# Handing the low parts of the output weights from VectorE to GpSimd, from weights that ScalarE scales in place

## The chip, the cores and the metric

The kernel runs on one core of a Trainium2 chip. The metric is the time of one launch on the device in microseconds (us); less is better. A core has TensorE (matrix products, PE in the profile; its weight loads are PEld), VectorE (DVE), ScalarE (ACT), GpSimd (POOL) and SyncE (SP), which here issues all DMA transfers.

## What is computed

One decoder layer over 2048 positions of width 1024, in float32: an RMSNorm, one input projection whose columns feed two groups of 512 channels, an output projection with residual, then a feed-forward block and a final RMSNorm.

```python
h = rmsnorm(x, norm_mix)
proj = h @ w_in                                 # x_lru, g_lru, v_cm, g_cm: 512 columns each
c = causal_depthwise_conv(x_lru, conv4_w, conv4_b)
y_lru = rg_lru(c, ...) * gelu(g_lru)            # gated linear recurrence over the positions
d = causal_depthwise_conv(v_cm * sigmoid(g_cm), dw31_w, dw31_b)
y_cm = silu(layernorm(d, cm_ln_g, cm_ln_b))
y = concat(rmsnorm(y_lru, out_norm_lru), rmsnorm(y_cm, out_norm_cm))
x = x + y @ w_out
h = rmsnorm(x, norm_ffn)
x = x + (silu(h @ w_gate) * (h @ w_up)) @ w_down
return rmsnorm(x, norm_final)
```

## The kernel before, in words

**Split products.** Every large product is made from operands split in two: a high part in the type fp32r, and a low part, the difference between the float32 value and the high part. `product` (L1328) adds three matmuls per chunk of 128 rows: high by high (L1334), high by low (L1335), low by high (L1336).

**Stages.** Stage 1 runs over 8 units (`UNITS`: two halves of 1024 positions by 4 blocks of 128 channels). A unit has two pairs of projections (`project`, 16 pairs in all, `PPAIRS`). For each pair SyncE loads raw weights into one of two buffers `w_raw`, ScalarE writes the high part (`split_hi`, L701) and GpSimd the low part (`split_lo`, L544). Around the projections: the short convolution and the gates (ScalarE, GpSimd), the recurrence as a scan (VectorE, `scan`, L1143), and the long convolution of 31 taps (VectorE, `conv31`, L1186), one instruction of 128x1024 per tap, whose running sum lies in PSUM. Stage 2 is the output projection: 16 row tiles of 128 positions, each in two groups (the LRU channels, then the others) of two PSUM banks with 12 matmuls each; the rows are added to the residual on VectorE (`add_row`, L1167), normed (`hn`, L1259) and transposed by TensorE (`turn_h2`, L1481). Stage 3 is the feed-forward block.

**The output weights.** They are four blocks (`WOQ`), n = 0 to 3, of 2 x 128 rows by 1024 columns, and use the same two buffers `w_raw` as pairs 16 to 19. `load_w_out` (L383, SyncE) waits until the low part of the block two before it is made (`s_wlo`). `w_out_hi` (L917, ScalarE) multiplies the raw rows by the gains of the output norms (`w_out_gain`) and writes `wo_hi`, one instruction per 128x1024. `w_out_lo` (L1157, VectorE) makes `raw * gain - wo_hi`, also one instruction per 128x1024. The kernel places the four calls by hand into the last long convolution, `conv31(7)`, ahead of the taps 12, 14, 17 and 19 (`W_OUT_AT`, L267). In the same convolution stand the scan of unit 6 (ahead of tap 11), `norm_centre(1)` (tap 16), and `add_row(0)` (tap 24).

**The order around it.** Each engine runs its instructions in the written order; a wait blocks all that is behind it.
ScalarE (L935 to L950): `w_out_hi(0)`, `w_out_hi(1)`, `gates(7)`, `y_split(0)` (high part of row tile 0 of y), `gate_functions(7)`, `w_out_hi(2)`, `two_minus(7)`, `w_out_hi(3)`, `squares_lru(1)`, `y_split(1)`, `squares_cm(1)`, `root(7)`, `y_split(2)`.
GpSimd (end of the loop at L620, then L649 to L659): `output(6)`, `gated_input(7)`, `y_lo_part(0)`, `decay(7)`, `decay_square(7)`, `y_lo_part(1)`, `scan_input(7)`, `fold(1, "var")` (L615, L617), `y_lo_part(2)`, `output(7)`, `fold(1, "cm")`. `decay` (L580) waits for the gate functions, `decay_square` (L585) for `two_minus`, `two_minus` for `decay`, `scan_input` (L603) for the root of ScalarE.
TensorE (L1475 to L1541): the gates of unit 7 in two tiles, `norm_mean(1)`, then for row tile 0: wait for the low part of y, wait for `s_wlo` 18 (weights' low parts of blocks 0 and 1), group 0, wait for `s_wlo` 20, group 1; then `norm_sums_lru(1)`, `norm_var(1)` (which waits for the fold), row tile 1, and `turn_h2(0)`, which waits for `hn(0)`.
VectorE behind `conv31(7)`: `scan(7)`, `norm_scale(1)`, `hn(0)`, `add_row(1)`.

Of the kernel before, what the change touches and what calls it, by code (L numbers as in the profile page):

```python
# [16 lines left out]
ALU = mybir.AluOpType  # L17
ACT = mybir.ActivationFunctionType
# [12 lines left out]
def hybrid_block(nc, x, norm_mix, w_in, conv4_w, conv4_b, gate_a_w, gate_a_b, gate_x_w, gate_x_b,  # L31
# [13 lines left out]
    UNITS = NH * NJ  # L45
    PPAIRS = 2 * UNITS
# [28 lines left out]
    with ExitStack() as ctx:  # L75
        base = (nc.sbuf_base + 63) // 64 * 64

        def at(name, shape, dt, offset):
            return nc.alloc_sbuf_tensor_at(name, shape, dt, offset=base + offset)

        def sem(name):
            return ctx.enter_context(nc.semaphore(name))
# [5 lines left out]
        wo_hi = at("wo_hi", [P, KD, D], F32R, 0)  # L88
        wo_lo = at("wo_lo", [P, KD, D], F32R, 32 * KIB)
# [19 lines left out]
        w_raw = [at(f"w_raw{s}", [P, 2, KD, P], F32, (128 + 8 * s) * KIB) for s in range(2)]  # L109
# [55 lines left out]
        def col(j, r):  # L165
            return par[:, j * NR + r:j * NR + r + 1]
# [6 lines left out]
        f32 = lambda ap: ap.bitcast(F32)  # L173
# [20 lines left out]
        s_whi = sem("w_hi_ready")  # L194
        s_wlo = sem("w_lo_ready")
# [68 lines left out]


        SCAN_AT, CENTRE_AT, LATE_AT = 22, 16, 27
        W_OUT_AT = (12, 14, 17, 19)  # L267
        CENTRE_AT_LAST, ROW0_AT = 16, 24
        X_NORM_AT = (7, 8, 9, 10, 12, 13, 14, 15)
        X_LO_AT = (9, 10, 11, 12, 14, 15, 16, 17)  # L270
# [27 lines left out]
        def yb(w):  # L298

            return w % 2 + 2 * (w // TPH)  # L300
# [9 lines left out]
        def w_out_gain(k):  # L310

            return col(k % NJ, R_ONL if k < NJ else R_ONC)
# [217 lines left out]
        def _(pool):  # L530
            g = nc.gpsimd
# [17 lines left out]
            def output(u):  # L549

                pool.wait_ge(s_h, u + 1)
                g.tensor_tensor(gel[u % 2][:, :], gel[u % 2][:, :], cv[u % 2][:, :], ALU.mult).then_inc(s_fin, 1)
# [21 lines left out]
            def gated_input(u):  # L574

                pool.wait_ge(s_ir, NS * (u + 1))
                pool.wait_ge(s_clo, u + 1)
                g.tensor_tensor(cv[u % 2][:, :], cv[u % 2][:, :], ib[:, :], ALU.mult).then_inc(s_ic, 1)

            def decay(u):  # L580

                pool.wait_ge(s_te, 2 * (u + 1))
                g.tensor_tensor(uw[:, :], uw[:, :], su[:, :], ALU.mult).then_inc(s_p, 1)

            def decay_square(u):  # L585

                pool.wait_ge(s_two, u + 1)
                g.tensor_tensor(su[:, :], su[:, :], uw[:, :], ALU.mult).then_inc(s_q, 1)
# [31 lines left out]
            for u in range(UNITS):  # L620
# [20 lines left out]
                if u >= 1:  # L641
                    output(u - 1)

            def y_lo_part(w):
                pool.wait_ge(s_yhi, w + 1)
                g.tensor_tensor(y_lo[yb(w)][:, :, :], y_raw[yb(w)][:, :, :], f32(y_hi[yb(w)][:, :, :]),
                                ALU.subtract).then_inc(s_ylo, 1)

            gated_input(UNITS - 1)  # L649
            pool.wait_ge(s_yst[0], 16 * UNITS // 2)  # L650
            y_lo_part(0)
            decay(UNITS - 1)
            decay_square(UNITS - 1)
            y_lo_part(1)
# [36 lines left out]
        def _(act):  # L691
            a = nc.scalar
            steps = [0]

            def step(ins):

                steps[0] += 1
                ins.then_inc(s_act, 1)
                act.wait_ge(s_act, steps[0])
# [124 lines left out]
            def gate_functions(u):  # L824

                j = u % NJ
                act.wait_ge(s_rr, NS * (u + 1))
                if u == 0:
                    act.wait_ge(s_rate, 3)
                a.activation(su[:, :], uw[:, :], ACT.Tanh, scale=rate[:, j:j + 1]).then_inc(s_te, 1)  # L830
                step(a.activation(uw[:, :], uw[:, :], ACT.Exp, scale=rate2[:, j:j + 1]))
                a.activation(uw[:, :], uw[:, :], ACT.Identity, bias=1.0).then_inc(s_te, 1)

            def two_minus(u):

                act.wait_ge(s_p, u + 1)
                a.activation(su[:, :], uw[:, :], ACT.Identity, scale=-1.0, bias=two[:, 0:1]).then_inc(s_two, 1)
# [79 lines left out]
            def w_out_hi(n):  # L917

                q = PPAIRS + n
                act.wait_ge(s_w[q % 2], 32 * (q // 2 + 1))  # L920
                if n == 0:
                    act.wait_ge(s_pair[3], PPAIRS)
                for e in range(2):
                    ins = a.activation(wo_hi[:, 2 * n + e], w_raw[q % 2][:, e].rearrange("p k c -> p (k c)"),
                                       ACT.Copy, scale=w_out_gain(2 * n + e))
                ins.then_inc(s_whi, 1)

            def y_split(w):
                act.wait_ge(s_yl[w % 2], 32 * (w // 2 + 1))
                if w >= 2:  # L930
                    act.wait_ge(s_out[3], w - 1)
                a.copy(y_hi[yb(w)][:, :, :], y_raw[yb(w)][:, :, :]).then_inc(s_yhi, 1)
# [4 lines left out]
            gates(UNITS - 1)  # L937
            act.wait_ge(s_fin, UNITS - 1)
            y_split(0)
            gate_functions(UNITS - 1)  # L940
            w_out_hi(2)
            two_minus(UNITS - 1)
            w_out_hi(3)
            squares_lru(1)
            y_split(1)
            squares_cm(1)
# [102 lines left out]
        def _(dve):  # L1049
            v = nc.vector  # L1050
            steps = [0]

            def step(ins):

                steps[0] += 1
                ins.then_inc(s_dve, 1)
                dve.wait_ge(s_dve, steps[0])
# [96 lines left out]
                    dve.wait_ge(s_h, u + 1)  # L1154
                    v.tensor_copy(hl[:, j:j + 1], cv[s][:, HALF - 1:HALF]).then_inc(s_hl, 1)

            def w_out_lo(n):  # L1157
                q = PPAIRS + n
                dve.wait_ge(s_whi, q + 1)
                for e in range(2):  # L1160
                    k = 2 * n + e
                    ins = v.scalar_tensor_tensor(out=wo_lo[:, k], in0=w_raw[q % 2][:, e].rearrange("p k c -> p (k c)"),  # L1162
                                                 scalar=w_out_gain(k), in1=f32(wo_hi[:, k]),
                                                 op0=ALU.mult, op1=ALU.subtract)
                ins.then_inc(s_wlo, 1)

            def add_row(w):  # L1167

                if w == 4:
# [16 lines left out]
            def conv31(u):  # L1186
                j = u % NJ
                t = glu[u % 2]
                last = 0
                for k in range(TAPS31):  # L1190
                    place = k
                    if u == NJ - 1:

                        for g in range(TPH):
                            if place == X_NORM_AT[g]:
                                x_norm(TPH + g)
                            if place == X_LO_AT[g]:
                                x_lo(TPH + g)
                    if place == CENTRE_AT and u == N0:
                        norm_centre(0, 6)  # L1200
                    if u >= 1 and place == (SCAN_AT_LAST if u == UNITS - 1 else SCAN_AT):
                        scan(u - 1)
                    if u == UNITS - 1 and place == ROW0_AT:
                        norm_rms(0)
                        add_row(0)
                    if u == UNITS - 1 and place == CENTRE_AT_LAST:
                        norm_centre(1, 6)
                    if u == UNITS - 1 and place in W_OUT_AT:
                        w_out_lo(W_OUT_AT.index(place))
                    if place == LATE_AT:  # L1210
                        if u == N0 + 1:
                            norm_scale(0)
                    if k == 0:
                        dve.wait_ge(s_glu, (NS + 1) * (u + 1))
                        if u >= 1:
                            dve.wait_ge(s_conv31, u)
                        ins = v.tensor_scalar(acc[:, :], t[:, 0:HALF], col(j, R_DW), col(j, R_DWB), ALU.mult, ALU.add)
                    else:
                        dve.wait_ge(s_dve, last)
                        if k == TAPS31 - 1 and u >= 2:  # L1220
                            dve.wait_ge(s_dst[u % 2], 16 * (u // 2))
                        into = dst[u % 2] if k == TAPS31 - 1 else acc
                        ins = v.scalar_tensor_tensor(out=into[:, :], in0=t[:, k:k + HALF], scalar=col(j, R_DW + k),  # L1223
                                                     in1=acc[:, :], op0=ALU.mult, op1=ALU.add)
                    if k == TAPS31 - 1:
                        ins.then_inc(s_conv31, 1)
                    else:
                        steps[0] += 1
                        last = steps[0]
                        ins.then_inc(s_dve, 1)  # L1230
            for u in range(UNITS):
                conv31(u)
# [11 lines left out]
            for w in range(NT):  # L1244
                i, g = w % TPH, w
# [11 lines left out]
                if w >= 2:  # L1257
                    dve.wait_ge(s_tr[1], w - 1)
                v.scalar_tensor_tensor(out=hn[w % 2][:, :], in0=x2[:, i], scalar=rstd[:, w:w + 1], in1=g_row[:, :],  # L1259
                                       op0=ALU.mult, op1=ALU.mult).then_inc(s_hn, 1)  # L1260
# [352 lines left out]
```

## Time and profile of the kernel before

| | |
|---|---|
| time, median of 3 runs | 2119.61 us (2119.1 to 2123.15) |
| time of the profiled execution | 2121.55 us |
| its span, first to last instruction | 2119.8 us |
| TensorE busy | 2056.3 us, 97% |
| VectorE busy | 927.3 us, 44% |
| ScalarE busy | 659.5 us, 31% |
| GpSimd busy | 674.2 us, 32% |
| mean granted TensorE clock | 0.987 |

The profiled execution is one run of the program; its own time is 1.75 us more than its span and 1.94 us more than the median. Busy times are sums over the whole span; the change touches about 60 us of it, from 434 to 500 us. A timeline row gives the start, the length from the first to the last instruction that it merges, engine, line, operation, output and inputs, how many were merged, and in brackets the idle time ahead of it with what ended that. In the chain of waits a row is start, length, engine, output and line. A granted clock of 1.00 is 2.4 GHz, 0.50 is 1.2 GHz.

### The profile page before, as it was taken

How to read it: one execution, taken by the hardware profiler on the slowest of the kernel's cores; microseconds unless marked ns; L12 is line 12 of the kernel's file. 1: busy time of each engine (PE TensorE's matmuls, PEld its weight loads, DVE VectorE, ACT ScalarE, POOL GpSimd, SP SyncE). 2: the span in 40 equal slices, each digit the busy share in tenths (PEclk: the TensorE clock that was granted, in tenths of full speed). 3: DMA queues.
4: the chain of work that ended last, by engine and by line, in shares of the span. 5: the costliest groups of instructions: out<-in, count | busy, mean ns of one | idle time of the engine just before them, and what ended most of it. 6: DMA issues, size and time to landing. Idle time of an engine off the chain costs nothing.

```text
span 2119.8 us, 22397 instructions
## 1 busy us (share of the span) xinstructions
PE 2056.3 (97%) x9130; PEld 1698.7 (80%) x9130; DVE 927.3 (44%) x1068; ACT 659.5 (31%) x792; POOL 674.2 (32%) x233
## 2 busy tenths in 40 slices
PE   6999999969999999999999999999999999999997
PEld 5887787847888888888888888888888888888886
DVE  5999899987644221222212222142222122221224
ACT  5466765664533111111121111231111111112112
POOL 2576559764523221212122121212212121211210
PEclk9999999979999999999999999999999999999999
DMA  5223232167853121111212121481211111121101
GB/s 157 58 79 101 80 99 61 59 208 246 250 170 95 44 60 40 44 55 40 59 40 59 40 59 40 139 277 40 59 40 58 41 41 58 40 59 40 40 0 79
DMA packets 189111, 172.42 MB, mean 81 GB/s; under 512 B 5854, under 2 KB 161502, under 8 KB 189066
## 3 DMA queue, kind: packets, MB, share of 16 engines
q1 hardware_dynamic: 189066, 171.81, 26.1%
q8 instruction: 29, 0.48, 0.1%
q14 instruction: 16, 0.13, 0.0%
HBM read 138.24 MB, written 33.55 MB: 81 GB/s over the span
## 4 chain that ended last, share of the span: by engine, by line
PE 90%; DVE 4%; POOL 2%; ACT 1%; issue 1%; DMA 1%; SPq 1%; DVEq 0%; POOLq 0%; ACTq 0%
PE ps L1334 26%; PE ps L1335 26%; PE ps L1336 26%; PE acc L1336 4%; PE acc L1335 4%; PE acc L1334 4%; DVE acc L1223 1%; PE ps L1359 1%; DVE wo_lo L1162 1%; PE ps L1490 1%; POOL w_lo L546 1%; DMA ny<-y_scr 0%; DVE cv L1151 0%; DVE nrs L1132 0%; DVE hn L1310 0%
## 5 line engine op out<-in xcount | busy, mean ns | idle before, releaser
L1334 PE MATMUL ps<-h_hi,wf_hi 128*128 128x512 f32 x1408 | 548.7, 390 | 0.0
L1336 PE MATMUL ps<-h_hi,wf_lo 128*128 128x512 f32 x1408 | 548.5, 390 | 0.0
L1335 PE MATMUL ps<-h_lo,wf_hi 128*128 128x512 f32 x1408 | 548.4, 390 | 0.0
L678 POOL TENSOR_TENSOR wf_lo<-w_raw,wf_hi 128x2048 fp32r<-128x2048 f32 x44 | 202.7, 4606 | 757.8 <-ACT wf_hi L958 757.8
L1280 DVE TENSOR_TENSOR act_gate<-act_gate,ps 128x512 f32<-128x512 f32 x88 | 60.5, 687 | 788.4 <-PE ps L1336 788.4
L1336 PEld LDWEIGHTS ps<-h_hi,wf_lo 128*128 128x128 f32 x1408 | 264.5, 188 | 54.6
L1334 PEld LDWEIGHTS ps<-h_hi,wf_hi 128*128 128x128 f32 x1408 | 264.5, 188 | 54.6
L1335 PEld LDWEIGHTS ps<-h_lo,wf_hi 128*128 128x128 f32 x1408 | 264.5, 188 | 54.6
L1223 DVE SCALAR_TENSOR_TENSOR acc<-glu,par,acc 128x1024 f32<-128x1024 f32 x232 | 299.0, 1289 | 7.2
L1025 ACT CAST f_hi<-act_gate 128x512 fp32r<-128x512 f32 x88 | 54.6, 620 | 495.8 <-DVE act_gate L1280 495.8
L674 POOL TENSOR_TENSOR wd_lo<-wd_raw,wd_hi 128x2048 fp32r<-128x2048 f32 x22 | 101.2, 4602 | 336.1 <-ACT wd_hi L964 336.1
L1334 PE MATMUL ps<-h_hi,w_hi 128*128 128x512 f32 x512 | 203.7, 398 | 4.2 <-POOL w_lo L546 2.6
L1298 DVE TENSOR_TENSOR x<-x,acc 128x512 f32<-128x512 f32 x176 | 120.1, 688 | 196.2 <-PE acc L1336 196.2
L1335 PE MATMUL ps<-h_lo,w_hi 128*128 128x512 f32 x512 | 201.3, 393 | 0.0
L1336 PE MATMUL ps<-h_hi,w_lo 128*128 128x512 f32 x512 | 201.1, 393 | 0.0
L964 ACT CAST wd_hi<-wd_raw 128x2048 fp32r<-128x2048 f32 x22 | 42.1, 1914 | 370.7 <-PE ps L1336 370.7
L1335 PE MATMUL ps<-wd_lo,f_hi 128*128 128x512 f32 x352 | 137.2, 390 | 0.0
L1334 PE MATMUL ps<-wd_hi,f_hi 128*128 128x512 f32 x352 | 137.1, 390 | 0.0
L1336 PE MATMUL acc<-wd_hi,f_lo 128*128 128x512 f32 x352 | 137.1, 390 | 0.0
L1336 PE MATMUL ps<-wd_hi,f_lo 128*128 128x512 f32 x352 | 137.1, 389 | 0.0
L1334 PE MATMUL acc<-wd_hi,f_hi 128*128 128x512 f32 x352 | 137.1, 389 | 0.0
L1335 PE MATMUL acc<-wd_lo,f_hi 128*128 128x512 f32 x352 | 137.0, 389 | 0.0
(170 smaller groups left out, 2745.0 us busy)
## 6 DMA issues: line engine op xcount, KB each, us to landing
w_raw<-in_w_gate SPq DMA_DIRECT2D x44, 512.0 KB, 4.1
w_raw<-in_w_up SPq DMA_DIRECT2D x44, 512.0 KB, 5.2
wd_raw<-in_w_down SPq DMA_DIRECT2D x22, 1024.0 KB, 4.8
w_raw<-in_w_in SPq DMA_DIRECT2D x32, 512.0 KB, 5.3
xt<-in_x SPq DMA_DIRECT2D x16, 512.0 KB, 3.8
x<-in_x SPq DMA_DIRECT2D x16, 512.0 KB, 6.6
out_block<-hn SPq DMA_DIRECT2D x16, 512.0 KB, 2.8
d_scr<-dst SPq DMA_DIRECT2D x8, 512.0 KB, 6.0
```

The lines of the kernel that those rows point to most:

```text
L546: g.tensor_tensor(w_lo[q % 2][:, :, :, :], w_raw[q % 2][:, :, :, :], f32(w_hi[q % 2][:, :, :, :]), ALU.subtract).then_inc(s_wlo, 1)
L674: g.tensor_tensor(wd_lo[:, :, :], wd_raw[:, :, :], f32(wd_hi[:, :, :]), ALU.subtract).then_inc(s_wdlo, 1)
L678: g.tensor_tensor(wf_lo[b][:, :, :, :], w_raw[b][:, :, :, :], f32(wf_hi[b][:, :, :, :]), ALU.subtract).then_inc(s_wlo, 1)
L964: a.copy(wd_hi[:, :, :], wd_raw[:, :, :]).then_inc(s_wdhi, 1)
L1025: a.copy(f_hi[b][:, st * TILE:(st + 1) * TILE], act_gate[n][:, :]).then_inc(s_fhi, 1)
L1162: ins = v.scalar_tensor_tensor(out=wo_lo[:, k], in0=w_raw[q % 2][:, e].rearrange("p k c -> p (k c)"), scalar=w_out_gain(k), in1=f32(wo_hi[ ...
L1223: ins = v.scalar_tensor_tensor(out=into[:, :], in0=t[:, k:k + HALF], scalar=col(j, R_DW + k), in1=acc[:, :], op0=ALU.mult, op1=ALU.add)
L1280: v.tensor_tensor(act_gate[n][:, :], act_gate[n][:, :], ps[2 * st + 1], ALU.mult).then_inc(s_free[2 * st + 1], 1)
L1298: v.tensor_tensor(x2[:, t, dh * TILE:(dh + 1) * TILE], x2[:, t, dh * TILE:(dh + 1) * TILE], ps[4 + bank], ALU.add).then_inc(s_outf[bank], 1)
L1334: pe.matmul(bank, lhs[0](c), rhs[0](c), start=first, stop=False)
L1335: pe.matmul(bank, lhs[0](c), rhs[1](c), start=False, stop=False)
L1336: mm = pe.matmul(bank, lhs[1](c), rhs[0](c), start=False, stop=last)
```

## The change

GpSimd makes the low parts of the output weights, each block in one subtraction of 128x2048. For that the gain has to be in the raw weights already: ScalarE scales each 128x1024 half of the block in place, waits for the second to be done (`step`), and then copies the whole block to `wo_hi`. The calls are placed anew: on GpSimd blocks 0 and 1 come behind `output(6)`, ahead of `gated_input(7)`, and blocks 2 and 3 behind `y_lo_part(0)`, ahead of `decay(7)`; on ScalarE `w_out_hi(2)` comes ahead of `gate_functions(7)` and `w_out_hi(3)` ahead of `two_minus(7)`. VectorE has none of them any more.

```diff
-        W_OUT_AT = (12, 14, 17, 19)
...
+            def w_out_lo(n):
+                q = PPAIRS + n
+                pool.wait_ge(s_whi, q + 1)
+                g.tensor_tensor(wo_lo[:, 2 * n:2 * n + 2], w_raw[q % 2][:, :].rearrange("p e k c -> p e (k c)"),
+                                f32(wo_hi[:, 2 * n:2 * n + 2]), ALU.subtract).then_inc(s_wlo, 1)
+
...
+            w_out_lo(0)
+            w_out_lo(1)
             gated_input(UNITS - 1)
             pool.wait_ge(s_yst[0], 16 * UNITS // 2)
             y_lo_part(0)
+            w_out_lo(2)
+            w_out_lo(3)
             decay(UNITS - 1)
             decay_square(UNITS - 1)
...
                 for e in range(2):
-                    ins = a.activation(wo_hi[:, 2 * n + e], w_raw[q % 2][:, e].rearrange("p k c -> p (k c)"),
-                                       ACT.Copy, scale=w_out_gain(2 * n + e))
-                ins.then_inc(s_whi, 1)
+                    rows = w_raw[q % 2][:, e]
+                    ins = a.activation(rows, rows, ACT.Copy, scale=w_out_gain(2 * n + e))
+                step(ins)
+                a.copy(wo_hi[:, 2 * n:2 * n + 2], w_raw[q % 2][:, :].rearrange("p e k c -> p e (k c)")).then_inc(s_whi, 1)
...
             y_split(0)
+            w_out_hi(2)
             gate_functions(UNITS - 1)
-            w_out_hi(2)
+            w_out_hi(3)
             two_minus(UNITS - 1)
-            w_out_hi(3)
             squares_lru(1)
...
-            def w_out_lo(n):
-                q = PPAIRS + n
-                dve.wait_ge(s_whi, q + 1)
-                for e in range(2):
-                    k = 2 * n + e
-                    ins = v.scalar_tensor_tensor(out=wo_lo[:, k], in0=w_raw[q % 2][:, e].rearrange("p k c -> p (k c)"),
-                                                 scalar=w_out_gain(k), in1=f32(wo_hi[:, k]),
-                                                 op0=ALU.mult, op1=ALU.subtract)
-                ins.then_inc(s_wlo, 1)
...
-                    if u == UNITS - 1 and place in W_OUT_AT:
-                        w_out_lo(W_OUT_AT.index(place))
```

## Rows read from the trace of the kernel before

**Rows 1.** The page, chain that ended last, by engine.
```profile
PE 90%; DVE 4%; POOL 2%; ACT 1%; issue 1%; DMA 1%; SPq 1%; DVEq 0%; POOLq 0%; ACTq 0%
```
**Rows 2.** The chain in order of time, 395 to 500 us, the low parts: start, length.
```profile
441.11 3.52 DVE wo_lo L1162 x2
...
447.17 5.40 DVE wo_lo L1162 x2
...
458.48 2.38 DVE wo_lo L1162 x2
...
463.39 3.52 DVE wo_lo L1162 x2
```
**Rows 3.** Timeline of TensorE: each restart from 442 us on.
```profile
442.13 0.77 PE L1334 MATMUL ps<-c_hi,gw_hi 128*128 128x512 f32 x1 [1.37 <-ACT uw L818]
...
452.71 0.77 PE L1334 MATMUL ps<-wo_hi,y_hi 128*128 128x512 f32 x1 [4.05 <-DVE wo_lo L1162]
...
466.96 0.80 PE L1334 MATMUL ps<-wo_hi,y_hi 128*128 128x512 f32 x1 [7.23 <-DVE wo_lo L1162]
...
478.67 1.33 PE L1385 MATMUL ps<-nsq,mean_w 128*128 128x512 f32 x2
...
494.69 1.09 PE L1490 MATMUL ps<-ident,hn 128*128 128x128 f32 x8 [2.38 <-DVE hn L1259]
```
**Rows 4.** Timeline of GpSimd, 435 to 473 us.
```profile
435.43 2.35 POOL L636 TENSOR_TENSOR c_lo<-cv,c_hi 128x1024 fp32r<-128x1024 f32 x1
440.01 2.35 POOL L552 TENSOR_TENSOR gel<-gel,cv 128x1024 f32<-128x1024 f32 x1 [2.23 <-DVE cv L1151]
...
466.46 2.69 POOL L607 TENSOR_TENSOR su<-su,cv 128x1024 f32<-128x1024 f32 x1 [1.83 <-ACT su L842]
...
471.56 1.28 POOL L617 TENSOR_TENSOR nsq<-nsq 128x512 f32<-128x512 f32 x1
```
**Rows 5.** Timeline of ScalarE, 434 to 460 us.
```profile
434.30 4.26 ACT L924 ACTIVATE wo_hi<-w_raw,par 128x1024 fp32r<-128x1024 f32 x4
...
445.07 0.69 ACT L822 ACTIVATE ib<-ps,par 128x512 f32<-128x512 f32 x1 [0.59 <-PE ps L1336]
...
446.59 1.15 ACT L830 ACTIVATE su<-uw,rate 128x1024 f32<-128x1024 f32 x1
...
451.20 2.17 ACT L924 ACTIVATE wo_hi<-w_raw,par 128x1024 fp32r<-128x1024 f32 x2
...
459.37 1.89 ACT L725 ACTIVATE ny<-ny 128x2048 f32<-128x2048 f32 x1
```
**Rows 6.** Groups of ScalarE, 0 to 440 us: busy us, mean ns of one.
```profile
L705 ACT CAST w_hi<-w_raw 128x2048 fp32r<-128x2048 f32 x16 | 30.4, 1900 | 0.5 <-DMA w_raw<-in_w_in 0.5
...
L924 ACT ACTIVATE wo_hi<-w_raw,par 128x1024 fp32r<-128x1024 f32 x4 | 4.3, 1137 | 0.0
```
**Rows 7.** Line L546 (`split_lo`), whole span: ns min/median/max.
```profile
L546 POOL TENSOR_TENSOR w_lo<-w_raw,w_hi x16: 4508/4625/6610, 14.8 to 391.0; 128x2048 fp32r<-128x2048 f32 x16
```
**Rows 8.** Timeline of SyncE's queue: the loads of output weight blocks 2 and 3.
```profile
444.67 8.73 SPq L388 DMA_DIRECT2D w_raw<-in_w_out  x4
```
**Rows 9.** Tile `w_raw`, 395 to 500 us: time from issue to landing.
```profile
DMA to landing us min/median/max: 3.2/3.9/5.4
```
**Rows 10.** Timeline of VectorE, 435 to 495 us.
```profile
435.50 4.43 DVE L1151 TENSOR_TENSOR_SCAN cv<-uw,hl,su 128x1024 f32<-128x1024 f32 x1 [9.87 <-POOL su L607]
...
466.83 6.58 DVE L1223 SCALAR_TENSOR_TENSOR acc<-glu,par,acc 128x1024 f32<-128x1024 f32 x5
...
485.33 2.35 DVE L1151 TENSOR_TENSOR_SCAN cv<-uw,hl,su 128x1024 f32<-128x1024 f32 x1
...
493.35 1.28 DVE L1259 SCALAR_TENSOR_TENSOR hn<-x,rstd,g_row 128x1024 f32<-128x1024 f32 x1
```
**Rows 11.** Stretches of 2 us: busy time by engine, then TensorE's granted clock.
```profile
455.00:457.00 2.00, 2.00 (x9) 1.66 (x8) 2.00 (x2) 0.99 (x1) 0.94 (x1) 0.87 0.97 361
...
471.00:473.00 2.00, 2.00 (x7) 1.60 (x6) 1.97 (x2) 0.00 (x0) 1.76 (x2) 0.60 0.00 0
```

## The prediction

> **What bounds the kernel now.** I read the page's chain first: TensorE holds 90% of it and VectorE 4% [rows 1], so the change can only matter where VectorE's share lies. The chain in order of time puts that at 435 to 495 us, between the last projection and the first output rows. There the four low-part blocks of the output weights stand in the chain itself, 3.52, 5.40, 2.38 and 3.52 us, 14.8 us together [rows 2]. But how much is it worth to TensorE? Its timeline [rows 3] answers: it waits 1.37 us for the gates, 4.05 us for the first two low parts (row tile 0, group 0 starts at 452.71), 7.23 us for the last two (group 1 starts at 466.96) and 2.38 us for `hn(0)` (494.69). From there TensorE is all but full, so what moves the transposes at 494.69 moves the end. These waits, 15.0 us, are the whole stake. At 478.67 stands a short product that does not wait now: `norm_var(1)`, which stands in TensorE's queue ahead of row tile 1 and needs the fold of the squares by GpSimd. That fold ended at 472.84 [rows 4], 5.8 us ahead of use.
>
> **The change, part by part.** All times are in the profiled execution (span 2119.8, its time 2121.55 us; the median of the runs is 2119.61, 1.9 us less).
>
> (a) VectorE loses eight instructions, 14.8 us. It is then ahead of what it needs, and waits at place 24 of the last long convolution for row tile 0.
>
> (b) ScalarE's block grows. Before, four scaled writes took 4.26 us for two blocks [rows 5], 2.1 each. Now each block is two scalings in place (the first passes after 1.04, the second must end, 1.14 [rows 6]) and a copy of 2048 columns, 1.90 [rows 6]: 4.1 us. An in-place scaling is not in the trace; between 0.95 (half of that copy) and 1.28 (a tap of VectorE on as many elements, rows 10) each; I take 1.14, the row on the same tile, and put the extra wait for its end at nothing beyond that. Blocks 0 and 1 run from 434.30 to 442.5 instead of 438.56, so the last unit's gates move by 2.5 us: their last read ended at 445.76 [rows 5], now 448.3. TensorE has 2.5 us more idle there and less behind it, so this costs nothing by itself.
>
> (c) GpSimd gets four subtractions of 2048 columns. The like one, `split_lo`, took 4.63 us in the median, 4.51 to 6.61 [rows 7]; I take 4.63, and 6.61 for the range. Its queue: `output(6)` ends at 442.36 [rows 4]; block 0 to 447.0; block 1 (ready 442.5) to 451.6; `gated_input(7)`, 2.35, to 454.0; `y_lo(0)` to 456.4. Group 0 of row tile 0 starts at 456.4 instead of 452.7 and ends after the same 6.9 us, at 463.3.
>
> (d) SyncE's queue: the load of block 2 waits for the low part of block 0, issued at 444.67 before [rows 8], at 447.05 now, second half at 447.5. A landing took 3.2 to 5.4 us, 3.9 in the median [rows 9]: block 2 lies there at 451.3. The load of block 3 follows block 1's low part at 451.6, lands near 456.4 and is hidden behind (e). The y and residual loads behind it start within 1 us of before.
>
> (e) The moved step. `w_out_hi(2)` now stands ahead of `gate_functions(7)`, and so waits in ScalarE's queue from 449.2 for the data: it runs from 451.3 to 455.4. The gate functions took 4.6 us from 446.59 to the next block at 451.2 [rows 5]; they end their turn at 460.0. `w_out_hi(3)` to 464.1. GpSimd subtracts block 3 to 468.8, so group 1 starts at 468.8, 1.8 us later than before, although TensorE idles 5.5 us rather than 7.2 in front of it.
>
> (f) What is queued behind the waiting subtraction on GpSimd: `decay(7)` and all after it. It now runs from 468.7 to 471.1 (2.35). `two_minus(7)` lets ScalarE reach `squares_lru(1)` at 472.2; from there to the end of the root it took 7.0 us (459.37 [rows 5] to 466.4, just ahead of `scan_input(7)` [rows 4]): 479.2. `scan_input(7)` takes 2.35 like the product at 440.01 (2.69 when it met VectorE [rows 4]): 481.6. The fold takes 3.7 (469.15 to 472.84): 485.3. `y_lo(1)` fits in between, done at 477.2, in time for row tile 1.
>
> (g) TensorE: group 1 and the sums behind it took 11.7 us (466.96 to 478.67); from 468.8 that ends at 480.6. Then it waits 4.8 us, where it waited nothing: `norm_var(1)` starts at 485.4. From there to the end of row tile 1 was 13.6 us (478.67 to 492.3): 499.0, and the transposes come straight behind, 4.3 to 4.4 us later than at 494.69.
>
> (h) VectorE: row tile 0's last sum ends 1.8 us later than 476.27; seven taps at 1.3 [rows 10] follow, 9.1 us, to 487.2. The scan (2.35) follows at once or behind `y_lo(2)` of GpSimd, which ends near 487.9; then reciprocal, scaling and `hn` took 7.0 us (487.68 to 494.63 [rows 10]): 497.3. That is 1.7 us ahead of TensorE, so VectorE's chain is covered; without that cover the cost would be +2.7.
>
> (i) The clock. After a stall TensorE was granted half speed for some time: 0.87 at 455 to 457 after the restart at 452.71, but 0.60 still at 471 to 473 after that at 466.96 [rows 11]. Row tile 1 restarts from a stall of 4.8 us now. Between the two restarts seen (about 6 and 12 slow products at 0.2 us extra each, against about as many as the first, which row tile 1 loses already) it loses from -0.2 to +1.2 us; I take +0.4, the middle.
>
> **Sum:** +4.35 +0.4 = +4.8 us: 2126.3 for the profiled execution, 2124.4 on the median. By stalls the same: 3.9 + 5.2 + 5.5 + 4.8 + 0 = 19.4 us against 15.0. Everything after 499 follows TensorE; the store of d and y and the loads of the next norm tile move by 2 to 3 us, less than TensorE.
>
> What of a rule against handing such work over? Here the row shows 4.63 us on GpSimd [rows 7] for what VectorE did in 2.38 when nobody disturbed it [rows 2]. The Trainium skill ("GPSIMD Engine Reference", Engine selection) keeps two-input elementwise work on VectorE, GpSimd being about half as fast; counted as engine time alone it would make the change 18.5 - 14.8 = 3.7 us slower, an estimate that ignores who waits. My sum does not use it.
>
> **Rivals.** (1) **VectorE's chain was the bound, and its 14.8 us come back.** For: rows 2 stand in the chain. Then the stalls for low parts and `hn(0)` go, 4.05 + 7.23 + 2.38 = 13.7 us: 2105.9. It decides only if the last low part is there before 461; against it, (e) puts it at 468.8. Half right (block 3 by 464) it gives no change. 5%.
> (2) **The fold is in time, or nearly.** Landing at 3.2 us, overlapped scalings, a copy faster than 1.90: VectorE's path (+2.7) or less sets the end, 2122.3 or down to 2119.6. The point is a fold that ends before 483.6. 17%.
> (3) **GpSimd and VectorE hold each other up.** The scan that takes 2.35 took 4.43 with GpSimd's `c_lo` beside it [rows 10, 4], and `split_lo` took 6.61 in 3 of its 16 runs [rows 7]. If block 0 and block 3 each take 6.61, the fold chain grows by 4.0: 2128.4; if one does, 2126.4. Against: VectorE has only convolution taps then, one operand of which is in PSUM, and five taps took 1.3 each beside `scan_input` and the fold [rows 10, 4]. 15%. The Trainium skill ("SBUF — State Buffer", on the two separate sides) has the shared port pair locked for a whole instruction by a VectorE operation with two SBUF inputs; by that rule the taps leave it free and the removed operations took it, so it would speak for 4.63 and for +4.8.
> (4) A larger clock loss or a late landing (5.4), +6 to +7: 2125.6 to 2126.6; in the main case's upper part.
>
> **How the numbers follow.** Main case 63%, from +3.4 to +7. A measurement here tells about 0.2% (4.2 us) from no change, and +4.8 lies hard by that edge: of the main case I count 38 points beyond it and 25 within. Rival 2 adds 17 within, rival 3 adds 15 beyond, rival 1 gives 4 faster and 1 within: slower 0.53, same 0.43, faster 0.04. The range takes in rival 2's half (+0.9) and rival 3 whole (+8.8): 2120.5 to 2128.4.
>
> **What would show each step.** Low parts of block 0 and 3 ending near 447 and 469; `w_out_hi(2)` waiting for DMA some 2 us; TensorE stalls of about 5.2, 5.5 and 4.8 us, the last released by the fold L617 and none, or a small one, for `hn`; VectorE idle some 13 us inside its last convolution. Wrong if the fold ends before 483, if the subtractions take over 5 us, or if `hn(0)` ends after row tile 1.

## The result

| | before | changed |
|---|---|---|
| median of 20 runs | 2120.73 us (2119.1 to 2123.95) | 2125.18 us (2122.7 to 2127.32) |
| ratio to before, 95% interval | | 1.0018 (1.0011 to 1.0024) |
| profiled execution: span | 2119.8 us | 2121.1 us |
| VectorE busy | 927.3 us | 914.5 us |
| ScalarE busy | 659.5 us | 667.2 us |
| GpSimd busy | 674.2 us | 687.6 us |

The changed kernel is slower by 0.18%, 3.8 us by the ratio and 4.45 by the medians. VectorE is relieved of 12.8 us, ScalarE gets 7.7 and GpSimd 13.4 more.

The two profiled executions already differ by 2.4 us before the stage begins: the scan of unit 6 ends at 439.93 us in the one [rows 10] and at 437.57 in the other. So every time below is counted from the end of that scan. The chain that ended last, by engine, first (page of the changed kernel; [rows 1] before):

```profile
PE 91%; POOL 3%; ACT 2%; DMA 1%; DVE 1%; issue 1%; SPq 1%; POOLq 0%; DVEq 0%; ACTq 0%
```

VectorE's share of the chain has fallen from 4% to 1%, GpSimd's has gone from 2% to 3% and ScalarE's from 1% to 2%. Where they hold TensorE shows in its timeline, which answers to [rows 3]:

```profile
442.22 0.77 PE L1332 MATMUL ps<-c_hi,gw_hi 128*128 128x512 f32 x1 [3.81 <-ACT uw L827]
...
453.88 0.77 PE L1332 MATMUL ps<-wo_hi,y_hi 128*128 128x512 f32 x1 [4.51 <-POOL y_lo L651]
...
466.51 0.80 PE L1332 MATMUL ps<-wo_hi,y_hi 128*128 128x512 f32 x1 [5.50 <-POOL wo_lo L646]
...
483.12 2.05 PE L1383 MATMUL ps<-nsq,mean_w 128*128 128x512 f32 x2 [5.43 <-POOL nsq L616]
...
497.12 1.03 PE L1488 MATMUL ps<-ident,hn 128*128 128x128 f32 x8
```

The stall of 7.23 us ahead of group 1 has shrunk to 5.50 and the one for `hn(0)`, 2.38, is gone. Those for the gates and for group 0 have grown, from 1.37 to 3.81 and from 4.05 to 4.51 us, and there is a new one of 5.43 us ahead of `norm_var(1)`, released by the last fold of GpSimd (L616). Together the four are 19.25 us, where the kernel before had 15.0. The queue of GpSimd (timeline of GpSimd, which answers to [rows 4]) tells why the fold is late:

```profile
439.99 9.01 POOL L646 TENSOR_TENSOR wo_lo<-w_raw,wo_hi 128x2048 fp32r<-128x2048 f32 x2
...
453.58 4.59 POOL L646 TENSOR_TENSOR wo_lo<-w_raw,wo_hi 128x2048 fp32r<-128x2048 f32 x1
461.96 4.50 POOL L646 TENSOR_TENSOR wo_lo<-w_raw,wo_hi 128x2048 fp32r<-128x2048 f32 x1 [3.79 <-ACT wo_hi L936]
466.42 2.36 POOL L582 TENSOR_TENSOR uw<-uw,su 128x1024 f32<-128x1024 f32 x1
...
476.97 2.37 POOL L606 TENSOR_TENSOR su<-su,cv 128x1024 f32<-128x1024 f32 x1 [1.79 <-ACT su L851]
...
481.71 1.26 POOL L616 TENSOR_TENSOR nsq<-nsq 128x512 f32<-128x512 f32 x1
```

`decay(7)` (L582) stands behind both subtractions and starts at 466.42. The block ahead of it was itself 3.79 us late for want of its high part, and ScalarE's timeline (which answers to [rows 5]) carries that on to the load:

```profile
431.95 2.17 ACT L934 ACTIVATE w_raw<-w_raw,par 128x1024 f32<-128x1024 f32 x2
434.15 1.90 ACT L936 CAST wo_hi<-w_raw 128x2048 fp32r<-128x2048 f32 x1
...
449.15 2.19 ACT L934 ACTIVATE w_raw<-w_raw,par 128x1024 f32<-128x1024 f32 x2 [2.38 <-DMA w_raw<-in_w_out]
...
453.18 1.15 ACT L839 ACTIVATE su<-uw,rate 128x1024 f32<-128x1024 f32 x1
...
457.78 2.17 ACT L934 ACTIVATE w_raw<-w_raw,par 128x1024 f32<-128x1024 f32 x2
...
468.82 1.15 ACT L846 ACTIVATE su<-uw,two 128x1024 f32<-128x1024 f32 x1 [6.93 <-POOL uw L582]
```

ScalarE waits 2.38 us for block 2 with the gate functions (453.18) queued behind, and 6.93 us for `decay(7)` with all the squares behind. VectorE (its timeline, which answers to [rows 10]) spends what it was given in waits for TensorE, the two that are shown and one of 1.98 us behind the second:

```profile
449.41 2.29 DVE L1136 TENSOR_TENSOR nd<-nd,ps 128x2048 f32<-128x2048 f32 x1 [5.35 <-PE ps L1383]
...
471.43 0.75 DVE L1182 SCALAR_TENSOR_TENSOR x<-ps,rms,x 128x512 f32<-128x512 f32 x1 [7.71 <-PE ps L1334]
...
483.97 3.46 DVE L1161 TENSOR_TENSOR_SCAN cv<-uw,hl,su 128x1024 f32<-128x1024 f32 x1
...
493.11 1.28 DVE L1257 SCALAR_TENSOR_TENSOR hn<-x,rstd,g_row 128x1024 f32<-128x1024 f32 x1
```

So `hn(0)` ends at 494.39, 2.7 us ahead of the transposes.

All kernels of this study, in us from the end of the scan of unit 6 (each a start in TensorE's timeline of its profiled execution, less the end of that scan), and the medians beside the before kernel's of the same chip:

| kernel | group 0 | group 1 | `norm_var(1)` | transposes 0 | transposes 1 | median | ratio to before (95%) |
|---|---|---|---|---|---|---|---|
| before | 12.8 | 27.0 | 38.7 | 54.8 | 66.6 | 2120.73 | 1 |
| changed | 16.3 | 28.9 | 45.6 | 59.6 | 71.3 | 2125.18 | 1.0018 (1.0011 to 1.0024) |
| e1_no_gain | 16.3 | 25.2 | 41.8 | 56.2 | 68.0 | 2120.14 | 0.9999 (0.9990 to 1.0008) |
| e2_var_later | 16.3 | 28.9 | 46.7 | 56.9 | 70.2 | 2124.20 | 1.0014 (1.0005 to 1.0023) |
| e3_more_gpsimd | 16.3 | 28.9 | 51.4 | 65.6 | 77.4 | 2130.16 | 1.0044 (1.0030 to 1.0058) |
| e4_scalar_only | 14.3 | 26.6 | 37.6 | 54.3 | 67.7 | 2121.57 | 1.0002 (0.9993 to 1.0011) |
| e5_order_mended | 16.3 | 28.3 | 40.1 | 53.6 | 65.4 | 2120.86 | 0.9993 (0.9984 to 1.0002) |
| e6_vector_places | 11.9 | 24.4 | 35.9 | 56.1 | 70.0 | 2122.63 | 1.0008 (0.9999 to 1.0017) |
| e7_rows_early | 11.9 | 24.4 | 35.8 | 49.8 | 65.7 | 2125.20 | 1.0016 (1.0007 to 1.0025) |
| e8_shared | 14.1 | 24.9 | 36.3 | 50.0 | 61.9 | 2116.90 | 0.9978 (0.9969 to 0.9987) |
| e9_row_at_24 | 16.3 | 28.3 | 39.1 | 54.9 | 66.7 | 2121.23 | 0.9999 (0.9990 to 1.0008) |

The kernel before had medians of 2120.51 beside e1 to e4, 2120.77 beside e5 to e7 and 2121.81 beside e8 and e9. A ratio is taken over all runs and is not the quotient of the two medians: e5's median lies above that of the kernel before it, its ratio below 1, since its eleven runs reach from 2116.01 to 2121.88 us.

### The profile page after: what moved, and what is told of

It reads as the page before. It is cut to its first block, busy times and chain, and to the rows that moved or that the text cites. A ratio compares the mean times of both kernels' runs of the same rounds, so it can differ in the third digit from the quotient of the medians.

```text
span 2121.1 us, 22397 instructions
## 1 busy us (share of the span) xinstructions
PE 2053.3 (97%) x9130; PEld 1695.1 (80%) x9130; DVE 914.5 (43%) x1060; ACT 667.2 (31%) x796; POOL 687.6 (32%) x237
## 4 chain that ended last, share of the span: by engine, by line
PE 91%; POOL 3%; ACT 2%; DMA 1%; DVE 1%; issue 1%; SPq 1%; POOLq 0%; DVEq 0%; ACTq 0%
PE ps L1332 26%; PE ps L1334 26%; PE ps L1333 26%; PE acc L1334 4%; PE acc L1333 4%; PE acc L1332 4%; PE ps L1357 1%; PE ps L1488 1%; POOL w_lo L545 1%; POOL wo_lo L646 0%; DMA ny<-y_scr 0%; POOL su L606 0%; SPq L356 0%; DVE hn L1308 0%; DVE x L1296 0%
## 5 line engine op out<-in xcount | busy, mean ns | idle before, releaser
L1334 PEld LDWEIGHTS ps<-h_hi,wf_lo 128*128 128x128 f32 x1408 | 264.4, 188 | 54.9
L1332 PEld LDWEIGHTS ps<-h_hi,wf_hi 128*128 128x128 f32 x1408 | 264.4, 188 | 54.8
L1031 ACT ACTIVATE act_gate<-ps 128x512 f32<-128x512 f32 x88 | 52.6, 598 | 268.9 <-PE ps L1334 268.9
```

The costliest lines, as they stand in the source:

```text
L1031: a.activation(act_gate[n][:, :], ps[2 * st], ACT.Silu).then_inc(s_free[2 * st], 1)
L1332: pe.matmul(bank, lhs[0](c), rhs[0](c), start=first, stop=False)
L1334: mm = pe.matmul(bank, lhs[1](c), rhs[0](c), start=False, stop=last)
```

## The experiments

**e1: the changed kernel without the scaling in place.** The gains of the output norms are left out of the output weights.

```diff
-                for e in range(2):
-                    rows = w_raw[q % 2][:, e]
-                    ins = a.activation(rows, rows, ACT.Copy, scale=w_out_gain(2 * n + e))
-                step(ins)
                 a.copy(wo_hi[:, 2 * n:2 * n + 2], ...)
```

> The changed kernel without the scaling in place: ScalarE only copies each block, so the gains of the output norms are left out of the output weights. Theory (the time is set by the chain load of block 2, block 2's high part, gate functions, block 3's high part, its low part on GpSimd, decay, squares, root, scan input, fold, norm_var): the scalings of blocks 2 and 3 are in that chain, 2.2 us each, so the time falls by 4.4 us from 2125.2 to about 2120.8, the level of the kernel before; from the end of the scan of unit 6 to the first transposes 55.1 us instead of 59.5. Rival (GpSimd's own 18 us of subtractions are the cost, ScalarE is hidden): stays at 2125. Rival (the block 0 and 1 scalings delay the gates and nothing else matters): below 1 us.

Measured: 2120.14 us, the level of the kernel before. In the stage 3.4 us went rather than 4.4: with ScalarE faster the two last blocks run back to back on GpSimd, which then sets the pace itself, so that `norm_var(1)` starts 3.8 us sooner; the last 0.4 us TensorE loses behind its longer stall (its timeline has 14.4 us from there to the transposes, 14.0 in the changed kernel). Group 0 starts at 16.3 us as in the changed kernel. GpSimd's timeline, and two restarts of TensorE:

```profile
453.76 9.15 POOL L646 TENSOR_TENSOR wo_lo<-w_raw,wo_hi 128x2048 fp32r<-128x2048 f32 x2
```
```profile
479.58 2.04 PE L1379 MATMUL ps<-nsq,mean_w 128*128 128x512 f32 x2 [6.53 <-POOL nsq L616]
...
493.93 1.03 PE L1484 MATMUL ps<-ident,hn 128*128 128x128 f32 x8
```

The fold is still what TensorE waits for. The scaling was in the chain, and the rival that ScalarE is hidden falls. So does the one that only the scalings of blocks 0 and 1 matter: it gave below 1 us.

**e2: `norm_var(1)` between the two groups of row tile 1.**

```diff
                     norm_sums_lru(1, 7)
-                    pe.wait_ge(s_dc, 2)
-                    norm_var(1, 6)
...
                     if group:
                         norm_steps(w)
+                    if group and w == 1:
+                        pe.wait_ge(s_dc, 2)
+                        norm_var(1, 6)
```

> The changed kernel with norm_var(1) moved in TensorE's queue from ahead of row tile 1 to between its two groups. Theory (the stall of 5.4 us is the fold ahead of row tile 1; next behind it is VectorE's hn(0), 2.7 us ahead): the stall at norm_var goes, the transposes wait for hn(0) instead, and the time falls by 2.7 us, to 2122.5. Rival (low parts late for group 1 set the time): no change, 2125. Rival (nothing behind the fold): falls by all of 5.4 us, to 2119.8.

Measured: 2124.20 us, 1.0 less than the changed kernel and not 2.7; the intervals of the two ratios overlap (1.0005 to 1.0023, 1.0011 to 1.0024), so the gain rests on the stage, where 1.1 us are left at the second transposes. The stall went where it was expected (timeline of TensorE):

```profile
486.07 1.02 PE L1383 MATMUL ps<-nsq,mean_w 128*128 128x512 f32 x2
...
496.30 1.97 PE L1488 MATMUL ps<-ident,hn 128*128 128x128 f32 x8 [3.73 <-DVE hn L1257]
```

The transposes start 2.7 us sooner, as worked out. But they take 1.97 us instead of 1.03, and from them to the next transposes TensorE needs 13.3 us instead of 11.7. The row of stretches of 2 us shows the granted clock at half there (the third number from the end, ahead of the DMA share and GB/s):

```profile
496.00:498.00 2.00, 1.70 (x9) 1.70 (x9) 2.00 (x4) 1.97 (x4) 0.00 (x0) 0.50 0.85 255
```

The stall that was moved here cost TensorE its clock behind it: 1.6 of the 2.7 us were given back so.

**e3: 128x1024 twice more on GpSimd, ahead of `decay(7)`.**

```diff
             w_out_lo(3)
+            pool.wait_ge(s_ic, UNITS)
+            for n in range(2):
+                g.tensor_tensor(c_lo[:, :], cv[(UNITS - 1) % 2][:, :], cv[(UNITS - 1) % 2][:, :],
+                                ALU.subtract).then_inc(s_more, 1)
+                pool.wait_ge(s_more, n + 1)
             decay(UNITS - 1)
```

> The changed kernel with two more subtractions of 128x1024 into a dead tile on GpSimd, behind the low part of block 3 and ahead of decay(7): 4.7 us. Theory (all that GpSimd does ahead of decay is paid in full through the fold): +4.7 us, 2129.9, and the stall ahead of norm_var grows from 5.4 to 10 us. Rival (the low part of block 3 and group 1 set the time, what comes behind it on GpSimd is covered): +0 to +1.

Measured: 2130.16 us, 5.0 more. The two took 3.87 us and not the 4.7 counted on (both inputs are one tile; that this is why was not tested), and the fold met VectorE's scan and took 3.12 us instead of 1.26. Those 3.87 us and the 1.86 more of the fold, 5.7 together, are what `norm_var(1)` starts later by (5.8). TensorE's wait is split in two, 2.03 us for the squares and 7.00 for the fold. Timelines of GpSimd and of TensorE:

```profile
467.63 3.87 POOL L664 TENSOR_TENSOR c_lo<-cv 128x1024 fp32r<-128x1024 f32 x2
...
486.90 3.12 POOL L617 TENSOR_TENSOR nsq<-nsq 128x512 f32<-128x512 f32 x1
```
```profile
477.11 6.05 PE L1397 MATMUL ps<-mean_w,ny 128*128 128x1 f32 x32 [2.03 <-ACT ny L740]
490.17 2.05 PE L1389 MATMUL ps<-nsq,mean_w 128*128 128x512 f32 x2 [7.00 <-POOL nsq L617]
```

Nothing was covered: group 1 starts at 28.9 as before, and all the rest is paid behind it. That the time hangs on what stands ahead of `decay(7)` is shown by this run.

**e4: ScalarE's whole part on the kernel before.** Scaling in place, block copy and ScalarE's new order; VectorE keeps the low parts at their places. The lines of the scaling and of the copy are those of the change.

```diff
...
-                    ins = v.scalar_tensor_tensor(out=wo_lo[:, k], in0=w_raw[q % 2][:, e]..., scalar=w_out_gain(k),
-                                                 in1=f32(wo_hi[:, k]), op0=ALU.mult, op1=ALU.subtract)
+                    ins = v.tensor_tensor(wo_lo[:, k], w_raw[q % 2][:, e]..., f32(wo_hi[:, k]), ALU.subtract)
...
             y_split(0)
+            w_out_hi(2)
             gate_functions(UNITS - 1)
-            w_out_hi(2)
+            w_out_hi(3)
             two_minus(UNITS - 1)
-            w_out_hi(3)
```

> ScalarE's whole part alone on the kernel before: scaling in place, copy of the block, and w_out_hi(2) and (3) ahead of the gate functions and of two_minus; VectorE keeps the low parts at their places, as plain subtractions of 128x1024. Theory (without GpSimd's subtractions ahead of decay, the fold ends near 475, ahead of its use at 478.7, and VectorE's convolution still sets hn(0)): no change within 1 us, 2120.7. Rival (ScalarE's longer and reordered queue is the cost): +3 to +4.5, 2124 to 2125.

Measured: 2121.57 us, ratio 1.0002, no change within the interval. Two restarts of TensorE:

```profile
476.20 2.06 PE L1385 MATMUL ps<-nsq,mean_w 128*128 128x512 f32 x2
...
492.91 1.97 PE L1490 MATMUL ps<-ident,hn 128*128 128x128 f32 x8 [3.31 <-DVE hn L1259]
```

`norm_var(1)` does not wait: the fold ends 36.1 us after the scan of unit 6, 3.2 later than before and 1.5 ahead of its use. So ScalarE's 8 us more and its new order are free as long as GpSimd goes on to `decay(7)` at once: the scaling costs only in company with GpSimd's subtractions (e1), which make it a part of the chain. One thing this run leaves out: `w_out_hi(2)` did not wait for its load here, as it did for 2.38 us in the changed kernel, since VectorE had block 0 done sooner and the load was issued sooner (4.7 us after the scan of unit 6, not 7.0). What that wait alone costs is not shown.

**e5: the change kept, its order mended.**

```diff
-            w_out_hi(2)
             gate_functions(UNITS - 1)
-            w_out_hi(3)
+            w_out_hi(2)
             two_minus(UNITS - 1)
+            w_out_hi(3)
...
+            decay(UNITS - 1)
             w_out_lo(2)
             w_out_lo(3)
-            decay(UNITS - 1)
...
-        CENTRE_AT_LAST, ROW0_AT = 16, 24
+        CENTRE_AT_LAST, ROW0_AT = 16, 30
```

> The change kept (scaling in place, low parts on GpSimd), its order mended: on ScalarE the gate functions stand ahead of w_out_hi(2) again and two_minus ahead of w_out_hi(3); on GpSimd decay(7) stands ahead of the low part of block 2; add_row(0) stands ahead of the last tap of the long convolution instead of tap 24. Theory (the cost is the order, through the fold): block 2 is loaded while the gate functions run, the fold ends near or before the sums of row tile 0, and the transposes start 53.4 us after the scan of unit 6 instead of 59.5: about 6 us less in the stage, 1.3 us less than the kernel before, 2119 to 2120 in all. Rival (GpSimd's subtractions, 4.5 us a block where VectorE takes 2.4, cannot be hidden in any order): 2123 or more.

Measured: transposes at 53.6 (53.4 expected), 2120.86 us (2119 to 2120 expected), ratio 0.9993. Two restarts of TensorE, neither of them waiting:

```profile
481.64 1.21 PE L1383 MATMUL ps<-nsq,mean_w 128*128 128x512 f32 x2
...
495.10 1.03 PE L1488 MATMUL ps<-ident,hn 128*128 128x128 f32 x8
```

The cost of the change is its order. GpSimd's 18 us are there in full and the 4 us are gone. How much of it is GpSimd's order and how much ScalarE's was not tested apart. A gain over the kernel before is not shown, since the interval reaches to 1.0002.

**e9: e5 with `add_row(0)` back ahead of tap 24** tells what the later row was worth.

```diff
-        CENTRE_AT_LAST, ROW0_AT = 16, 30
+        CENTRE_AT_LAST, ROW0_AT = 16, 24
```

> The kernel of e5_order_mended with add_row(0) back ahead of tap 24. Theory (with the fold in time VectorE's path from row tile 0 over seven taps, scan and norm to hn(0) is the next bound): TensorE waits for hn(0) some 2.6 us and restarts at half clock, 2122 to 2124. Rival (VectorE has time enough since it makes no low parts): as e5_order_mended, 2119.5 to 2121.

Measured: 2121.23 us, ratio 0.9999, between the two. The order alone, without the later row, so takes the cost away. TensorE waits for `hn(0)`, but 2.15 us and at full clock:

```profile
495.91 1.09 PE L1488 MATMUL ps<-ident,hn 128*128 128x128 f32 x8 [2.15 <-DVE hn L1257]
```

The mechanism is right and worth 1.3 us in the stage (54.9 against 53.6), at least: group 1 and the sums behind it took 1.0 us less here than in e5 (10.8 and 11.8), with fewer products at half clock. The clock that I added to the stall is not right. In the time the two runs can't be told apart.

**e6: VectorE's low parts moved, in the kernel before.**

```diff
-        W_OUT_AT = (12, 14, 17, 19)
-        CENTRE_AT_LAST, ROW0_AT = 16, 24
+        W_OUT_AT = (13, 13, 16, 16)
+        CENTRE_AT_LAST, ROW0_AT = 15, 24
...
-            two_minus(UNITS - 1)
             w_out_hi(3)
+            two_minus(UNITS - 1)
```

> The kernel before, with VectorE's low parts placed where GpSimd is idle or both high parts are there: blocks 0 and 1 ahead of tap 13, blocks 2 and 3 ahead of tap 16, norm_centre(1) ahead of tap 15, and w_out_hi(3) ahead of two_minus on ScalarE. Theory (5.2 of VectorE's 14.8 us were waits for GpSimd's instructions, and the group 1 stall was the late load of block 3): group 1 starts near 459 instead of 467, VectorE ends about 4.3 us earlier, hn(0) still ends last, 2116.2. Rival (the low parts take 14.8 us wherever they stand): within 1 us of 2120.5.

Measured: 2122.63 us, ratio 1.0008 (0.9999 to 1.0017); a miss, of the rival too. Group 1 starts 2.6 us sooner, not 8, but VectorE gains nothing (one group of its timeline, and a restart of TensorE):

```profile
453.31 9.09 DVE L1162 SCALAR_TENSOR_TENSOR wo_lo<-w_raw,par,wo_hi 128x1024 fp32r<-128x1024 f32 x4
```
```profile
494.16 1.97 PE L1491 MATMUL ps<-ident,hn 128*128 128x128 f32 x8 [6.50 <-DVE hn L1260]
```

Four instructions in a row that would take 4.8 us alone (2.38 for two [rows 2]) took 9.09: `decay_square` and `y_lo(1)` of GpSimd came between them, and took 2.52 and 3.07 us instead of 2.35. The waits for GpSimd were not at the old places, they follow the instructions. And the longer stall cost TensorE its clock.

**e7: e6, with `norm_scale(1)`, `hn(0)` and `add_row(1)` inside the last long convolution.**

```diff
+                    if u == UNITS - 1 and place == 28:
+                        norm_scale(1)
+                        hn_row(0)
+                    if u == UNITS - 1 and place == 30:
+                        add_row(1)
...
             load_y(3)
+            store_swish(1)
             store_d(UNITS - 1)
```

> The kernel of e6_vector_places, with norm_scale(1) and hn(0) ahead of tap 28 and add_row(1) ahead of tap 30 of the last long convolution on VectorE, and the store of the swish of norm tile 1 issued ahead of the stores of unit 7. Theory (with the low parts early, TensorE waits for hn(0) alone): the transposes of row tile 0 follow row tile 1 at once, 7 to 9 us less than the kernel before, 2112 to 2114. Rival (the later scan of unit 7 delays the second half's norms, or the loads of row tile 4, and the gain is given back by 600 us): 2116 or more.

Measured: 2125.20 us, ratio 1.0016; the rival, and 11 to 13 us above the theory. The transposes start at 49.8, 5 us sooner than before, and all of it and more is gone by the third ones: 84.1 us after the scan (524.28) against 80.2 before (520.13). TensorE's timeline has the new waits, GpSimd's has the load behind the last:

```profile
493.29 0.64 PE L1342 MATMUL ps<-wo_hi,y_hi 128*128 128x512 f32 x1 [2.17 <-DVE x L1182]
...
508.15 0.50 PE L1342 MATMUL ps<-wo_hi,y_hi 128*128 128x512 f32 x1 [1.21 <-POOL y_lo L646]
...
516.25 1.10 PE L1393 MATMUL acc<-nsq,mean_w 128*128 128x512 f32 x2 [1.57 <-POOL nsq L617]
```
```profile
512.40 2.37 POOL L615 TENSOR_TENSOR nsq<-nd 128x1024 f32<-128x1024 f32 x1 [4.30 <-DMA ny<-y_scr]
```

The loads of that norm tile were issued 64.1 us after the scan of unit 6, against 53.4 before, because the scan of unit 7 and the stores behind it came 10.7 us later. The three waits are 5.0 of the 8.8 us lost from the first transposes to the third. Most of the rest is clock: behind the first and the last of them some eight products each ran at half speed, about 0.2 us longer (granted 0.50 at 494 to 496 and at 518 to 520 us).

**e8: mended order, and the low parts shared.** GpSimd makes blocks 0 and 2, VectorE 1 and 3, from the weights scaled in place; each low part also waits for the one before it. The edit is shown against e5.

```diff
+        W_OUT_AT = {15: 1, 21: 3}
...
             gate_functions(UNITS - 1)
             w_out_hi(2)
+            w_out_hi(3)
             two_minus(UNITS - 1)
-            w_out_hi(3)
...
             w_out_lo(0)
-            w_out_lo(1)
...
             decay(UNITS - 1)
             w_out_lo(2)
-            w_out_lo(3)
             decay_square(UNITS - 1)
...
+            def w_out_lo(n):
+                q = PPAIRS + n
+                dve.wait_ge(s_whi, q + 1)
+                dve.wait_ge(s_wlo, q)
+                v.tensor_tensor(wo_lo[:, 2 * n:2 * n + 2], w_raw[q % 2][:, :].rearrange("p e k c -> p e (k c)"),
+                                f32(wo_hi[:, 2 * n:2 * n + 2]), ALU.subtract).then_inc(s_wlo, 1)
```

> The mended order, and the four low parts shared: GpSimd makes blocks 0 and 2, VectorE blocks 1 and 3 (one subtraction of 128x2048 each, ahead of taps 15 and 21), each where the other engine has just ended its own; w_out_hi(3) stands ahead of two_minus. Theory (TensorE is held by the last low part of each group; VectorE has free time and takes 2.4 us where GpSimd takes 4.5): group 1 starts 23.3 us after the scan of unit 6 (before 27.0, changed kernel 28.9), the transposes about 48.6 us after it (before 54.8), and the time is 2115 to 2117. Rival (the two engines block each other at both places and VectorE's chain to hn(0) grows): 2119 or more.

Measured: 2116.90 us beside 2121.81 for the kernel before, ratio 0.9978 (0.9969 to 0.9987): 0.22% faster than the kernel before, and faster than the changed one too (1.0018). The stage is 1.4 us longer than worked out. VectorE's timeline, then TensorE's:

```profile
460.91 2.29 DVE L1191 TENSOR_TENSOR wo_lo<-w_raw,wo_hi 128x2048 fp32r<-128x2048 f32 x1 [1.77 <-POOL wo_lo L648]
```
```profile
463.25 0.80 PE L1342 MATMUL ps<-wo_hi,y_hi 128*128 128x512 f32 x1 [5.08 <-DVE wo_lo L1191]
...
488.33 1.09 PE L1498 MATMUL ps<-ident,hn 128*128 128x128 f32 x8
```

Each of VectorE's low parts starts as soon as GpSimd's has ended, takes 2.29 us, and nothing comes in between; the instructions of GpSimd that started beside them took 3.21 and 4.13 us instead of 2.35. How much of the gain over e5 is the sharing, how much `w_out_hi(3)` ahead of `two_minus`, and what two half instructions in place of each one would do, was not tested. The gain keeps to the end: at the second transposes it is 4.7 us, and so it is in the ratio.

## Why the prediction was right

It said 2124.4 us (2120.5 to 2128.4), and of the stage 4.8 us more; measured were 2125.18 us and 4.8 us (59.6 against 54.8). Its likeliest case held, step by step, in us from the end of the scan:

| step | predicted | measured |
|---|---|---|
| group 0 starts (c) | 16.5 | 16.3 |
| ScalarE starts on block 2 (d) | 11.4 | 11.6 |
| group 1 starts (e) | 28.9 | 28.9 |
| `norm_var(1)` starts (f, g) | 45.5 | 45.6 |
| `hn(0)` ends (h) | 57.4 | 56.8 |
| transposes start (g, i) | 59.5 | 59.6 |

- (a) The 14.8 us came back to VectorE and were spent waiting, 5.35, 7.71 and 1.98 us. The first of these waits is for `norm_centre(1)` at tap 16, which the prediction does not have; the others are at place 24, as it says. Some 13 us of idle time were forecast.
- (b) An in-place scaling takes 1.14 us on average and the copy 1.90, 4.07 for a block; the extra wait for its end is some 0.03. That it is 4.4 us dearer in the chain than no scaling was tested by e1; there GpSimd gives out first, so 3.4 show in the stage. The prediction booked the scaling's delay of the gates at nothing by itself: e4, where they move as far, bears it out.
- (c) The subtractions took 4.50 to 4.59 us, so 4.63 was right and 6.61 did not come. The rival of the two engines holding each other up falls for the changed kernel: VectorE's taps averaged 1.288 us from 395 to 500 us (35 of them; 1.287 and 36 before), and none beside the subtractions took over 1.29. The Trainium skill ("SBUF — State Buffer", on the two separate sides) says that only VectorE operations with two SBUF inputs, or in a two-port mode, take the pair shared with GpSimd; by that rule, and by these rows, the trace agrees.
- (e), (f) The wait of `w_out_hi(2)` for its load was 2.38 us (2.1 worked out), that ahead of `norm_var(1)` 5.43 (4.8): the fold ended at 45.4 as forecast, and group 1 and its sums took 0.5 us less (11.2, not 11.7), which the wait took up. The chain through `decay`, the root and the fold is shown by e3 (work put into it is paid in full) and by e9 and e5 (taken out of it, the loss is gone). That the gate functions behind the load are a part of it is read from the rows only.
- (i) From the start of `norm_var(1)` to the transposes went 14.0 us with no wait among them; before it was 16.0 with one of 2.38, 13.6 without. So TensorE lost 0.4 us more to its clock; the middle of a range from -0.2 to +1.2 was taken, and that it fell on 0.4 is luck.
- By stalls the prediction has 3.9 + 5.2 + 5.5 + 4.8 = 19.4 us; measured were 3.81 + 4.51 + 5.50 + 5.43 = 19.25. It has the length of group 0 as 6.9 us, where its rows give 7.0 (452.71 to 459.73); nothing hangs on that.
- The sum of the time: 4.7 us at the second transposes, 3.8 in the ratio. 0.7 of the rest shows between the fifth and the sixth transposes, 14.4 us before and 13.7 in the changed kernel: a wait of 0.56 us for a fold of a later norm tile that the kernel before has there is gone. "Everything after 499 follows TensorE" was that much too strong.
- The chances: 0.53 for slower by over 0.2% and 0.43 for within. The 0.18% measured lies on that edge, where the prediction said it would, and just inside, so not on the side that got the larger chance. The edge itself was too wide: 20 runs of each kernel gave an interval from 0.11 to 0.24%, clear of no change.

What was not in the prediction is how little is between such orders: of the rivals, VectorE's relief giving 13.7 us was out of reach (group 1 hangs on low parts that GpSimd makes one after the other), but e8 shows that 4.7 us of it were to be had. The 1.2 us of e5 show in the stage alone.

## What to carry to other kernels

When work is handed to an idle engine, cost the queue and not the engine: follow what stands behind each handed instruction to the first use by the bound engine, and compare that slack (5.8 us here) with how much later the last of it ends (12.5 us: the fold ended 32.9 us after the scan of unit 6 before, and 45.4 in the changed kernel). An instruction that waits for a transfer is better kept behind work that is ready (gate functions ahead of `w_out_hi(2)`, a part of e5 that was not tested by itself). And share a burst of two-input work between VectorE and GpSimd block by block, one large instruction each, rather than giving it all to one: that order (e8) was the only one of these that beat the kernel before clear of noise.

## What the runs showed of the hardware

- The clock after a stall of TensorE ahead of the first transposes: after 2.38 us (before) and 2.15 us (e9) the eight transposes took 1.09 us, full speed; after 3.31 (e4), 3.73 (e2) and 6.50 us (e6) they took 1.97 us, at a granted clock of 0.50 (in stretches of 2 us; 1.00 in the first two). Ahead of each of these stalls TensorE had multiplied without a pause, for at least the last 6 us at full clock. The distance to the next transposes was 11.8 to 11.9 us in the first two and 13.3 to 13.9 in the others. So the three longer stalls cost 1.5 to 2.1 us each on top of themselves. The length of the stall alone does not decide: in e7 TensorE was at half clock right behind a stall of 2.17 us (493.29; ahead of it eight transposes and a wait of 0.43 us) and soon behind one of 1.57 us (516.25; ahead of it eight products with one column), and in e1 it kept full clock after 1.62 us (462.96).
- VectorE instructions with both inputs in SBUF, side by side with GpSimd's, took turns with them: four of 1.2 us took 9.09 us in e6, and two took 4.53 us in e4 (460.59). In e8 one of 128x2048 took 2.29 us, and GpSimd's beside it waited (3.21 and 4.13 us instead of 2.35).
- A GpSimd subtraction whose two inputs are the same tile took 1.90 us for 128x1024 (e3), against 2.35 for two tiles.
